# The opening of a two-layer diffusion trunk: modulation in halves, x1 turned by a diagonal product, two sums of blocks by DMA

## The reference

```
sh_m, sc_m, gt_m, sh_f, sc_f, gt_f = split(silu(c) @ ada_w[i] + ada_b[i], 6)
h  = rms_norm(x, g0) * (1 + sc_m) + sh_m
y  = pool_mixer(h)       # window means of 2, 4, 8, 16 tokens minus h, four groups of 256
                         # channels, each times its own 256 x 256 matrix, times pool_scale
x1 = x + gt_m * rms_norm(y, g1)
h  = rms_norm(x1, g2) * (1 + sc_f) + sh_f
x2 = x1 + gt_f * rms_norm(square(relu(h @ w1)) @ w2, g3)
```

## Time and profile before

| | us |
|---|---|
| median of 3 runs | 940.53 (940.26 to 940.94) |
| profiled execution, its own time | 941.23 |
| its span, first to last instruction | 939.1 |
| TensorE busy | 916.6 |
| VectorE / ScalarE / POOL busy | 652.8 / 430.9 / 45.2 |

### The profile page before, as it was taken

How to read it: one execution, slowest core, us unless ns; L and a number is a source line. 1 busy time by engine, 2 the same in 40 slices (tenths; PEclk the granted TensorE clock), 3 DMA queues, 4 the chain that set the end, 5 groups by cost and what they waited for, 6 DMA issues and landing times. The chain is left out here.

```text
span 939.1 us, 11422 instructions
## 1 busy us (share of the span) xinstructions
PE 916.6 (98%) x4623; PEld 755.0 (80%) x4623; DVE 652.8 (70%) x627; ACT 430.9 (46%) x523; POOL 45.2 (5%) x77
## 2 busy tenths in 40 slices
PE   8889999999999999999999999999999999999996
PEld 6658877888888888889888888898888888888885
DVE  6786299489578866686667644857856873793688
ACT  6654474445246333264322224555534534543463
POOL 3002000010001001000101000000000000000000
PEclk9999999999999999999999999999999999999999
DMA  9999349626834585424655531183870662175124
GB/s 304 349 350 345 141 139 291 243 65 187 291 113 113 161 336 205 132 61 172 221 181 208 180 128 52 59 300 101 258 262 21 181 201 75 60 211 176 40 52 179
DMA packets 89819, 167.71 MB, mean 179 GB/s; under 512 B 4222, under 2 KB 34018, under 8 KB 89768
## 3 DMA queue, kind: packets, MB, share of 16 engines
q1 hardware_dynamic: 83912, 155.25, 48.4%
q0 software_dynamic: 5856, 11.75, 6.0%
HBM read 160.66 MB, written 6.32 MB: 178 GB/s over the span
## 5 line engine op out<-in xcount | busy, mean ns | idle before, releaser
L669 PE MATMUL ps<-in_hi,w_parts 128*128 128x512 f32 (+1 forms) x784 | 290.0, 370 | 0.9 <-DVE in_lo L1594 0.5
L671 PE MATMUL ps<-in_hi,w_parts 128*128 128x512 f32 (+1 forms) x784 | 288.0, 367 | 0.0
L670 PE MATMUL ps<-in_lo,w_parts 128*128 128x512 f32 (+1 forms) x784 | 288.0, 367 | 0.0
L1417 DVE TENSOR_TENSOR w_parts<-raw,w_parts 128x2048 fp32r<-128x2048 f32 x81 | 185.5, 2291 | 126.2 <-ACT w_parts L1097 126.1
L1097 ACT ACTIVATE w_parts<-raw 128x2048 fp32r<-128x2048 f32 x81 | 154.8, 1911 | 213.3 <-PE ps L671 193.3
L669 PEld LDWEIGHTS ps<-in_hi,w_parts 128*128 128x128 f32 x784 | 147.7, 188 | 29.5 <-issue 3.3
L671 PEld LDWEIGHTS ps<-in_hi,w_parts 128*128 128x128 f32 x784 | 147.7, 188 | 24.4
L670 PEld LDWEIGHTS ps<-in_lo,w_parts 128*128 128x128 f32 x784 | 147.8, 188 | 24.1
L669 PE MATMUL ps<-w_parts,ops_hi 128*128 128x512 f32 x280 | 109.3, 390 | 2.3 <-DVE y L1469 0.9
L670 PE MATMUL ps<-w_parts,ops_hi 128*128 128x512 f32 x280 | 109.0, 389 | 0.0
L671 PE MATMUL ps<-w_parts,ops_lo 128*128 128x512 f32 x224 | 87.1, 389 | 0.0
(11 more groups left out here) (198 smaller groups left out, 1039.4 us busy)
## 6 DMA issues: line engine op xcount, KB each, us to landing
raw<-in_ffn_w_dram SPq DMA_DIRECT2D x57, 1024.0 KB, 5.4
ada_raw<-in_ada_w_dram SPq DMA_DIRECT2D x56, 512.0 KB, 6.3
xs<-in_ffn_w_dram SPq DMA_DIRECT2D x14, 1024.0 KB, 5.4
raw<-in_conv_in_w_dram SPq DMA_DIRECT2D x16, 512.0 KB, 5.2
xs<-in_ffn_w_dram POOLq DMA_DIRECT2D x7, 1024.0 KB, 8.5
raw<-in_ada_w_dram SPq DMA_DIRECT2D x4, 1024.0 KB, 11.7
ada_sum<-in_ada_w_dram SPq DMA_DIRECT2D x4, 1024.0 KB, 12.3
win<-in_ada_w_dram SPq DMA_DIRECT2D x4, 1024.0 KB, 11.7
```

Of the source, the lines that this page charges most:

```text
L669: nc.tensor.matmul(o, hi, b_hi, start=start, stop=False, skip_group_check=on)
L670: nc.tensor.matmul(o, hi, b_lo, start=False, stop=False, skip_group_check=on)
L671: return nc.tensor.matmul(o, lo, b_hi, start=False, stop=stop, skip_group_check=on)
L1417: nc.vector.tensor_tensor(w_lo[:, u % W_SLOTS, :], raw_of(u), w_hi[:, u % W_SLOTS, :].bitcast(F32), ALU.subtract).then_inc(w_lo_ready, 1)
```

## The change

- The 20 modulation loads hold the same bytes in other cuts: for shift and scale together 256 rows by 512 columns of each (2 KB rows, two DMAs), four loads for channels 0 to 511 (`M_SUMS[0]`), four for the rest, and the same for the MLP's (`F_SUMS`); the gate is 256 rows by all 1024 columns (4 KB rows), its bias added by a product. There are eleven places; the two new ones lie under `in_hi`.
- `columns` makes four chunks at once. The gate is weighed as four rows (`weigh_gate`), spread by four products (`spread_gate`) and applied by tiles of tokens (`token_gate`).
- x1 isn't normalized: `first_diag` puts 1/rms on a diagonal, and `turn_chunk`, a plain f32 product of x1 with it, turns and scales at once: six chunks for each tile, chunks 3 and 7 later (`turn_rest`). The MLP's first products then have all 512 tokens.
- N and S of the first seven are added up by DMAs from POOL, which accumulate (`add_first_parts`), and SP's two waits for `make_part` in `load` go.
- ScalarE's list follows: `pool_input` 0 to 3 after the first `copy_sums`, 4 to 7 after the second; `split_hi(1)` after the gate's root; the four `first_root` in a row, then `copy_sums(F_SUMS[0])`, `copy_first(4)` and `(5)`, `first_hi` 0 to 3, `split_hi(2)`, `copy_first(7)`, `split_hi(3)`, `copy_sums(F_SUMS[1])`, `first_hi` 4 to 7. `load(1)` comes after 12 modulation loads, `load(2)` after 16, `load(3)` after 20.

```diff
+PRE = [("m", h, kk) for h in range(2) for kk in range(4)] + [("g", 0, kk) for kk in range(4)] + [("f", h, kk) for h in range(2) for kk in range(4)]
+PRE_LOADS = 4
+M_SUMS, GATE_SUM, F_SUMS = (0, 1), 2, (3, 4)
+SUMS_BANK = (2, 3, 2, 3, 3)
+PRE_SLOTS = (4, 5, 9, 10, 0, 1, 2, 3, 6, 1, 2, 3, 1, 2, 3, 7, 8, 1, 2, 3)
...
+                what, h, kk = PRE[i]
+                rows = ada_rows(0)[:, 2 * kk:2 * kk + 2, :]
+                if what == "g":
+                    sp.dma_start(pre_slot(i), rows[:, :, GATE_M * D:(GATE_M + 1) * D]).then_inc(pre_in[PRE_SLOTS[i]], 16)
+                else:
+                    first = SHIFT_M if what == "m" else SHIFT_F
+                    for s in range(2):
+                        sp.dma_start(pre_slot(i)[:, :, s, :], rows[:, :, (first + s) * D + h * H:(first + s) * D + (h + 1) * H]).then_inc(pre_in[PRE_SLOTS[i]], 16)
...
+                if what == "g":
+                    if first:
+                        pe.wait_ge(gate_row_in, 16)
+                        for j in range(4):
+                            nc.tensor.matmul(ps[32 * j:32 * (j + 1), sums_bank(n), 0:Q], ones[0:1, 0:32], gate_row[0:1, quarter(j)], start=True, stop=False)
+                    for k in range(2):
+                        for j in range(4):
+                            mm = nc.tensor.matmul(ps[32 * j:32 * (j + 1), sums_bank(n), 0:Q], silu_wide[:, 2 * kk + k, :], pre_slot(i)[:, k, quarter(j)],
+                                                  start=False, stop=last and k == 1)
+                else:
+                    for j in range(4):
+                        mm = nc.tensor.matmul(ps[32 * j:32 * (j + 1), sums_bank(n), :], silu_wide[:, 2 * kk + j % 2, :], pre_slot(i)[:, j % 2, j // 2, :],
+                                              start=first, stop=last)
                 mm.then_inc(ada_done, 1)
...
+            def spread_gate():
+                pe.wait_ge(gate_sums, 1)
+                pe.wait_ge(pool_diff, BAND_CHUNK + 2)
+                for j in range(4):
+                    mm = nc.tensor.matmul(ps[:, 6 + j // 2, (j % 2) * Q:(j % 2 + 1) * Q], ident[:, 32 * j:32 * j + 1].to_broadcast([P, P]), g_four_rows, start=True, stop=True)
                 mm.then_inc(ada_turned, 1)
...
+            def turn_chunk(t, c):
+                return nc.tensor.matmul(ps[:, FIRST_BANK[c], toks(t)], xs[:, t, c * P:(c + 1) * P], y_tok[:, t, 0:P], start=True, stop=True)
+            def turn_first(t):
+                pe.wait_ge(x1_diag, t + 1)
+                pe.wait_ge(y0_gated, NT)
+                pe.wait_ge(y0_copied, GROUPS)
+                pe.wait_ge(pool_diff, NC)
+                for c in FIRST_AT_ONCE:
+                    tr = turn_chunk(t, c)
                 tr.then_inc(x1_turned, 1)
+            def turn_rest(c):
+                pe.wait_ge(f_made, 1 if c == 3 else 2)
+                for t in range(NT):
+                    tr = turn_chunk(t, c)
+                tr.then_inc(x1_turned, 1)
             def start_pairs():
...
+                def chunk(k):
+                    pe.wait_ge(f_lo, k + 1)
                     need_weights(1)
-                    for k in (2 * pair, 2 * pair + 1):
-                        for m in range(4):
-                            last = feat_products(1, k, m, 0, k, COLS, toks(2 * side, 2), k == 0 and side == 0, False)
+                    for m in range(4):
+                        last = feat_products(1, k, m, 0, k, COLS, ALL, k == 0, False)
                     return last
...
+                chunk(0)
+                turn_rest(3)
+                chunk(1)
+                turn_rest(7)
+                chunk(2)
+                chunk(3).then_inc(unit_done, 1)
+                add_up(16)
+                add_up(17)
+                pe.wait_ge(xt_copied, len(FIRST_COPIED))
                 second_unit(2)
-                turn_up(11)
+                add_up(18)
+                add_up(19)
                 second_unit(3)
-                part(1, 1).then_inc(unit_done, 1)
-                pe.wait_ge(cols_read, cols_value(len(SUMS) - 1))
+                turn_up(F_SUMS[1])
                 second_unit(0)
-                need_weights(3)
-                third_unit(2)
+                pe.wait_ge(cols_read, cols_value(F_SUMS[1]))
                 second_unit(1).then_inc(unit_done, 1)
-                third_unit(3)
-                need_weights(4)
-                for m in range(4):
-                    for k in range(UK):
-                        last = feat_products(4, k, m, 1, UK + k, COLS, ALL, False, k == UK - 1)
-                    last.then_inc(bank_done, 1)
+                for u in (3, 4):
+                    need_weights(u)
+                    for m in range(4):
+                        for k in range(UK):
+                            if m == 0:
+                                pe.wait_ge(f_lo, UK + k + 1)
+                            last = feat_products(u, k, m, u - 3, UK + k, COLS, ALL, False, k == UK - 1)
+                        last.then_inc(bank_done, 1)
...
-            pe.wait_ge(silu_ready, 2)
+            pe.wait_ge(silu_ready, 1)
             add_up(0)
             window(4)
             add_up(1)
             window(5)
-            turn_up(0)
+            add_up(2)
             window(6)
-            add_up(2)
+            add_up(3)
+            turn_up(M_SUMS[0])
             window(7)
-            add_up(3)
-            turn_up(1)
+            add_up(4)
             need_weights(POOL_U)
             pe.wait_ge(row_wide, 1)
             pe.wait_ge(vec_ready, 1)
             pool_group(0)
-            add_up(4)
             add_up(5)
-            turn_up(2)
             add_up(6)
             pool_group(1)
             add_up(7)
-            turn_up(3)
+            turn_up(M_SUMS[1])
             add_up(8)
+            add_up(9)
             pool_group(2)
-            add_up(9)
-            turn_up(4)
-            pool_group(3)
-            turn_up(5)
             add_up(10)
             add_up(11)
-            turn_up(6)
-            turn_up(7)
-            add_up(PRE_F)
-            add_up(PRE_F + 1)
-            stay_busy(0, 6)
-            turn_up(8)
+            pool_group(3)
+            spread_gate()
+            add_up(12)
+            add_up(13)
+            stay_busy(5, 6)
+            add_up(14)
+            stay_busy(5, 6)
+            turn_first(0)
+            turn_first(1)
+            turn_first(2)
+            add_up(15)
+            stay_busy(5, 6)
+            turn_up(F_SUMS[0])
+            turn_first(3)
+            stay_busy(5, 6)
             ffn(0)
...
                 operand_lo(layer, q, R)
                 if (layer, q) == (0, 0):
-                    make_part(layer, q, N)
                     operand_sum(layer, q, Q_)
                     operand_lo(layer, q, N)
...
+            def token_gate(t):
+                dve.wait_ge(ada_turned, GATE_SUM + 1)
+                dve.wait_ge(y0_sq, NT * (GROUPS - 1) + t + 1)
+                yt = y_tok[:, t, :].rearrange("p (a n) -> p a n", a=2)
+                nc.vector.tensor_tensor(yt, yt, ps[:, 6:8, :], ALU.mult).then_inc(y0_gated, 1)
...
+            def first_diag(t):
                 dve.wait_ge(x1_rms, t + 1)
                 nc.vector.reciprocal(st0[:, 7, t:t + 1], st0[:, 6, t:t + 1]).then_inc(x1_rcp, 1)
                 dve.wait_ge(x1_rcp, t + 1)
-                nc.vector.tensor_scalar(y_tok[:, t, :], xs[:, t, :], st0[:, 7, t:t + 1], None, ALU.mult).then_inc(x1_norm, 1)
...
+            def copy_sixth():
+                dve.wait_ge(x1_turned, NT)
+                nc.vector.tensor_copy(xt[:, 6, :], ps[:, FIRST_BANK[6], :]).then_inc(x6_copied, 1)
...
-            columns(0)
+            columns(M_SUMS[0])
             diff(0)
             diff(1)
             split_lo(POOL_U)
             diff_lo(0)
+            diff(2)
             diff_lo(1)
-            columns(1)
-            diff(2)
+            diff(3)
             diff_lo(2)
-            diff(3)
+            diff_lo(3)
             group_out(0)
-            columns(2)
-            diff_lo(3)
+            group_out(1)
+            columns(M_SUMS[1])
             diff(4)
             diff(5)
-            group_out(1)
             diff_lo(4)
-            columns(3)
+            diff(6)
             diff_lo(5)
-            gate_copy(0)
-            diff(6)
             diff(7)
             diff_lo(6)
             diff_lo(7)
             group_out(2)
-            gate_copy(1)
-            group_gate(0)
-            split_lo(1)
+            weigh_gate()
             group_out(3)
-            group_gate(1)
-            gate_copy(2)
+            token_gate(0)
+            token_gate(1)
             dve.wait_ge(y0_sq, NT * GROUPS)
             nc.vector.tensor_tensor(st_y[:, :, 0:2], st_y[:, :, 0:2], st_y[:, :, 2:4], ALU.add).then_inc(y0_sum, 1)
             dve.wait_ge(y0_sum, 1)
             nc.vector.tensor_tensor(st0[:, 2, :], st_y[:, :, 0], st_y[:, :, 1], ALU.add).then_inc(y0_sum, 1)
-            gate_copy(3)
```

(85 more changed lines are left out.)

295 lines of the change are left out of this document (102 added, 193 removed).

## The result

The changed kernel takes 955.15 us (median of 4 runs, 953.59 to 956.09) against 940.39 beside it: ratio 1.0145 as recorded, interval 1.013 to 1.016, so slower. (The quotient of the two medians is 1.0157, 14.8 us.) The profiled execution took 955.66 with a span of 953.9.

The account below looks back on a forecast made before the run. TensorE's queue was taken to bound the kernel from 61 us on. MLP start +15.2, work to the seven -1.2, sums -1.9, set-up -0.1 give +12.0 us on the median 940.53: 952.5, range 945 to 959.

Parts of the forecast that it names:

- rival B: In the opening, half clock after TensorE's idle times doubles group 0 (+3.0) and some turns (+2): 957.5; chance 0.20.
- if half clock shows before group 0: Sign ahead of the first pool group: TensorE at half clock there would make the prediction wrong and point to rival B.
- Up to pool group 0: First modulation: columns at 26.4, 4.8 us late; pool group 0 at 33.8, with TensorE idle for 4.8 us before it.
- The pool groups: Four groups of pool products in the opening, priced at 3.04 us each; group 3 ends at 58.0, 7.4 late.
- The turns: Turning x1 ahead of the MLP by f32 products with the diagonal: 0.275 us each, 1.75 a tile; bounds 0.15 and 0.45.
- Rival C: Turns of x1 at a transpose's price (0.15), fillers and turn_up also cheap: +5 to +9, middle 948; chance 0.19.
- First MLP product to the seven: TensorE's own work from first MLP product to first of the seven: 51.8 us instead of 53.04, 1.2 less.
- The longer rows: Modulation loads in the opening: some 400 GB/s instead of 349, 2.6 us a megabyte; without that, 0.8 us worse.
- rival A: The load stream bound the opening: MLP starts 5.6 us earlier, before 70.6, total 931.8; chance 0.08.
- The sums: Two sums of blocks by DMA leave VectorE in the first seven products: 1.9 us saved; bounds 0 and 3.
- Rival D: POOL's sums come late and TensorE waits for N or S: the 1.9 saved turns into +2, 956.4; chance 0.05.
- The doubled price: In the first seven, a sum by DMA within SBUF could take double: 144 against a need at about 142, costing some 2.

Follow-up runs that it names:

- e2: The changed kernel with filler products (results unread) added in TensorE's holes of the opening: 951.6 us, ratio 1.0107.
- e7: The changed kernel with the reordered opening, tile 3 turned right behind the others, and fillers in the remaining holes: 943.81 us, ratio 1.0020.
- e4: The changed kernel with all modulation loads cut into pieces of 256 columns, rows of 1 KB: 956.73 us, ratio 1.0157.
- e12: e7 with the modulation weights fetched in rows of 1 KB instead of 2 and 4 KB: 946.29 us, ratio 1.0048.
- e1: The kernel before with only the two sums of blocks moved from VectorE to accumulating DMAs on POOL: 938.3 us, ratio 0.9977.
- e3: The changed kernel with add_up(15) before the first turn, six fillers removed and tile 3 turned before turn_up: 949.38 us, ratio 1.0087.
- e5: The changed kernel with the opening's queues reordered, the second modulation half's add_ups moved ahead of pool groups 0 and 1: 950.09 us, ratio 1.0087.
- e8: The changed kernel with x1's turns as transposes of a tile normalized by VectorE, as in the kernel before: 954.78 us, ratio 1.0134.
- e10: e7 with x1's turns as transposes of a tile normalized by VectorE, as in the kernel before: 947.26 us, ratio 1.0062.
- e6: The changed kernel with both new orders, the opening's of e5 and tile 3's of e3, without added fillers: 947.53 us, ratio 1.0061.

## Why the prediction was right, and where a step was off

952.5 was forecast with 945 to 959; 955.15 was measured. One part of the mechanism held: the opening became later because halves put more in front of each stage, and two smaller gains stand against it. The clock was left out of the sum, though it was written down as rival B, and by the prediction's own sign ("if half clock shows before group 0") B came true: 0.54 from 28 to 30 us, 0.50 in group 0. 955.15 lies about midway between the forecast and B's 957.5. Part of the nearness is luck. The forecast is a span of 939.1 + 12.0 = 951.1; e2, the same kernel with the clock at 1.00, has 948.5, and the changed kernel 953.9. So the work was put 2.6 us too high and the clock at nothing, where it cost 5.4 between these two executions and 3.5 between the medians. Forecast and changed kernel, mark by mark:

| mark | forecast | trace |
|---|---|---|
| columns | 26.4 | 26.61 |
| pool group 0 begins | 33.8 | 33.73 |
| second columns | 44.7 | 46.7 |
| group 2 begins | 49.8 | 51.71 |
| group 3 ends | 58.0 | 61.1 |
| first turn | 68.9 | 72.17 |
| three tiles turned | 74.15 | 78.0 |
| tile 3 turned | 79.5 | 82.7 |
| first MLP product | 82.7 | 86.54 |
| first of the seven | 134.5 | 138.58 |
| from there to the end | 816.5 | 815.3 |

- **Up to pool group 0** the walk down the queues is right to 0.2 us. The idle time before it is 3.74 and not 4.8, since the add_up at 28.08 ran at half clock (1.90 us long).
- **The pool groups are the mis-sized term.** Each was priced at 3.04, full clock. Group 0 took 5.1 and group 2 4.6: 3.6 us, of which 3.1 are left where group 3 ends. Rival B, group 0 doubled and some turns, was given 0.20; it did happen, and group 2 and the first MLP products with it, which B did not have. e2 shows that it is the clock and that idle time has to do with it: fillers alone bring both groups back to 3.1.
- **The turns.** 0.275 with the seam was taken for a product, 1.75 us for a tile; at full clock the trace shows 1.42 for the six of tile 3 (81.26 to 82.68) and 0.20 each for four (94.42 to 95.22). The first three tiles took 5.8 us nevertheless, at 0.57, and 4.5 at full clock in e2. So the price was 0.8 too high and the clock cost 1.4. Rival C had the direction right and its price (0.15) too low, and its sum of +5 to +9 is missed even with the clock held (e2: +10.1).
- **First MLP product to the seven:** 51.8 forecast, 52.04 measured; in e7 50.64. Here too half clock at the start hides that the estimate was 1.1 too high: the first twelve products take 4.25 us (86.54 to 90.79), where 12 x 0.2275 = 2.73 was reckoned.
- **The longer rows** were put at 0.8 us. e4 shows 1.6 (not resolved), e12 2.5 where TensorE hardly waits for anything else, a lower clock included. The stream is not what bounds the changed kernel, and rival A is out: with 383 to 388 GB/s the first MLP product came at 86.54, not before 70.6. The Trainium skill (DMA: Bandwidth & Descriptors, Specifications) would have rows from 512 B up at line rate; the rows of 1 KB here moved 348 GB/s and the longer ones up to 396, so the measurement decides against it.
- **The sums** were put at 1.9; 2.2 alone (e1), 1.7 to 2.0 in e7. They come in time: DMAs from POOL were issued at 115.99, 125.19 and 138.32 us, and TensorE has no wait between 138.5 and 220. Rival D is out. The doubled price that the forecast feared could have been ruled out ahead: the seven DMAs of the earlier trace rows are those of `add_part`, which accumulate too.
- **The spread.** "0.07%" for the kernel before came from three runs. In 44 later ones it took 939.6 to 945.8 us, so that differences of 2 us between small groups of runs are at the edge.

The difference by parts, by ratios: +13.6 in all; 11.7 of it (11.3 by the medians) go with another order and fillers (e7), without taking any part of the change back. In the profiled executions e7's span is 2.9 above the kernel before: +1.6 for a later first turn, +6.8 for all tokens' turns ahead of the first chunk, -2.4 from there to the seven, -3.2 behind it (rounded). So most of the loss was not the new work, but the holes in its order and the clock that fell around them. How it divides between the two is known only for the fillers (3.5, e2): the gains of e3 and e5 hold both. What fillers would give the kernel before, which has a clock of 0.50 from 61 to 64 us itself, was not tried.

## What to carry to other kernels

When stages are made coarser, walk the new order down each queue and look for the engine's holes. Put work that is due later into a hole before it is filled with anything else. Price the products behind a hole at both clocks, and let the forecast be a sum of both: group 0, behind a hole of 3.7 us, took 5.1 us in one kernel and 4.3 in another. Test an edit that trades one engine for another (here VectorE's normalizing for dearer products) in a version where its neighbours don't wait: the same edit showed nothing in e8 and 3.5 us in e10. And look at the granted clock of both before giving the whole difference to the edit.

## What was not expected of the hardware

- The clock fell before the long hole, not in it: granted 1.00 from 20 to 28 us, when TensorE was busy 7.19 of 8 us, and 0.54 from 28 to 30, when it was busy 1.99 of 2. It was still 0.50 in group 0, 3.7 us of idle time later. In e5, busy for 4.18 of the 6 us from 24 to 30, it stayed at 1.00; in e6, with the same instructions up to there, it fell again. Why it falls at 28 in some executions stays open; that fillers before and in the holes go with 1.00 all through the opening is what e2 and e7 show.
- The time of one kernel goes with its granted clock from run to run. The kernel before took 939.6 us at a clock of 0.997 and 945.8 at 0.991, its extremes in 44 runs; e5 took 948.1 at 0.997 and 951.8 at 0.991. With fillers in all holes the clock is high in each run (e7: 0.995 to 0.998, 943.2 to 945.2 us). Differences between single profiles, as e8's 2.4 us, aren't to be trusted.
- An accumulating DMA of 1 MB from POOL takes no double time. The seven of `add_part` in the kernel before land after 8.2 to 8.7 us, the two for N in the changed kernel after 8.5 and 8.9. A plain load of 1 MB by SP takes 5.4 in the median of the kernel before, but 8.3 in the changed kernel between 105 and 150 us, where those two for N run.
